# Sixteen projection quads in another matmul form: hi and lo of the activations in one matmul

## What is computed

```python
h = rmsnorm(x, g_pre_mix)
proj = h @ w_in                      # nq, nkv, ngate, rq, rk, rv, rg, mq, bg
mem_n = rmsnorm(mem, g_mem)
mkv = (mem_n @ w_mem_kv)             # memory keys and values
y_c = memory_attention(mq, mk, mv)   # 4 heads of 256
y_a = nsa_attention(q, kv, gates, ...)  # 8 heads of 128: compressed, selected, window
y_b = retention(q_r, k_r, v_r) * silu(rg)
merged = sum of sigmoid(bg[n]) * (y_n @ w_br_n)
x = x + rmsnorm(merged @ w_o, g_post_mix)
h2 = rmsnorm(x, g_pre_ffn)
x = x + rmsnorm((gelu(conv(h2 @ w_gate)) * conv(h2 @ w_val)) @ w_down, g_post_ffn)
```

## Time and profile before

| | us |
|---|---|
| median of 3 runs (lowest, highest) | 1719.74 (1719.73, 1719.93) |
| the profiled execution | 1719.76 |
| its span, first to last instruction | 1717.6 |
| PE busy with matmuls | 1703.9 |
| DVE busy | 1123.0 |
| ACT busy | 817.8 |

### The profile page before, as it was taken

How to read it: one execution, slowest core, us unless ns; L and a number is a source line. 1 busy time by engine, 2 the same in 40 slices (tenths; PEclk the granted TensorE clock), 3 DMA queues, 4 the chain that set the end, 5 groups by cost and what they waited for, 6 DMA issues and landing times.

```text
span 1717.6 us, 26440 instructions
## 1 busy us (share of the span) xinstructions
PE 1703.9 (99%) x9582; PEld 1494.4 (87%) x9582; DVE 1123.0 (65%) x1488; ACT 817.8 (48%) x1105; POOL 48.7 (3%) x53
## 2 busy tenths in 40 slices
PE   9999999999999999999999999999999999999997
PEld 9998999999888888888888888888888888888886
DVE  7645567666575554554565777776776776776777
ACT  7433345444344444444444565455455454454453
POOL 1000000000140000000000010000000000000000
PEclk9999999999999999999999999999999999999999
DMA  9566478444655666666657466666665666656654
GB/s 298 187 222 205 137 224 250 129 136 139 214 165 176 197 187 195 220 196 196 184 183 244 163 195 195 187 196 188 190 193 183 189 196 187 192 188 191 196 175 144
DMA packets 245992, 327.79 MB, mean 191 GB/s; under 512 B 12907, under 2 KB 167308, under 8 KB 245388
## 3 DMA queue, kind: packets, MB, share of 16 engines
q1 hardware_dynamic: 245900, 326.47, 61.0%
HBM read 321.71 MB, written 3.67 MB: 189 GB/s over the span
## 4 chain that ended last, share of the span: by engine, by line
PE 96%; DVE 1%; ACT 1%; issue 1%; DMA 1%; POOL 0%; POOLq 0%; DVEq 0%; SPq 0%; ACTq 0%
PE bank L1430 18%; PE bank L1421 15%; PE bank L1420 15%; PE bank L1422 15%; PE bank L1434 9%; PE bank L1394 4%; PE bank L1396 4%; PE bank L1395 4%; PE bank L1407 1%; PE bank L1409 1%; PE bank L1408 1%; PE bank L1728 0%; PE bank L1707 0%; PE bank L1646 0%; PE bank L1628 0%
## 5 line engine op out<-in xcount | busy, mean ns | idle before, releaser
L880 DVE TENSOR_TENSOR wlo<-wraw,whi 128x1024 fp32r<-128x1024 f32 x580 | 709.8, 1233 | 416.4 <-ACT whi L599 414.4
L599 ACT ACTIVATE whi<-wraw 128x1024 fp32r<-128x1024 f32 x580 | 611.9, 1059 | 653.4 <-PE bank L1422 378.3
L1430 PE MATMUL bank<-hx,whi 128*128 128x512 f32 x1376 | 344.6, 392 | 0.6 <-DVE wlo L880 0.5
L1430 PEld LDWEIGHTS bank<-hx,whi 128*128 128x128 f32 x1376 | 248.0, 189 | 45.9 <-issue 0.7
L1434 PEld LDWEIGHTS bank<-hx,wlo 128*128 128x128 f32 x1376 | 187.7, 190 | 13.4
L1434 PE MATMUL bank<-hx,wlo 128*128 128x256 f32 x1376 | 191.9, 282 | 0.0
L1420 PE MATMUL bank<-whi,hx 128*128 128x512 f32 x448 | 175.7, 392 | 0.0
L1422 PE MATMUL bank<-whi,hx 128*128 128x512 f32 x448 | 174.4, 389 | 0.0
L1421 PE MATMUL bank<-wlo,hx 128*128 128x512 f32 x448 | 174.3, 389 | 0.0
L1420 PE MATMUL bank<-whi,r_hi 128*128 128x512 f32 x384 | 149.8, 390 | 0.0
L1421 PE MATMUL bank<-wlo,r_hi 128*128 128x512 f32 x384 | 149.5, 389 | 0.0
(11 more groups left out here) (267 smaller groups left out, 2176.4 us busy)
## 6 DMA issues: line engine op xcount, KB each, us to landing
wraw<-in_w_in SPq DMA_DIRECT2D x200, 512.0 KB, 3.8
wraw<-in_w_up SPq DMA_DIRECT2D x176, 512.0 KB, 4.4
wraw<-in_w_down SPq DMA_DIRECT2D x88, 512.0 KB, 4.0
wraw<-in_w_mem_kv SPq DMA_DIRECT2D x32, 512.0 KB, 4.2
wraw<-in_w_o SPq DMA_DIRECT2D x32, 512.0 KB, 4.4
wraw<-in_w_br_mem SPq DMA_DIRECT2D x16, 512.0 KB, 4.3
wraw<-in_w_br_nsa SPq DMA_DIRECT2D x16, 512.0 KB, 4.5
wraw<-in_w_br_ret SPq DMA_DIRECT2D x16, 512.0 KB, 4.4
```

What stands on the lines that cost most here:

```text
L599: nc.scalar.activation(whi[:, c], wraw[:, c], ACT.Copy).then_inc(hi_done, 1)
L880: V.tensor_tensor(wlo[:, c], wraw[:, c], whi[:, c].bitcast(F32), ALU.subtract).then_inc(lo_done, 1)
L1430: T.matmul(ps[UP_PAIRS[j][t]][:, :], whi[:, c, k, t * P:(t + 1) * P], hx[:, :, k0 + k, :], start=first and k == 0, stop=False, skip_group_ ...
```

## The change

The sixteen quads of `mq`, `mk`, `nq`, `kv0` and of the second kv quad in `mix` go from `chunk_t` to a new `chunk_d`, which is `chunk_u` with the bank pair and the activations as arguments. The memory's hi and lo activations get one common tensor, `mx`. Each quad now takes a pair of banks. Their evacuation goes from `by_column` to `by_column_wide`, with a copy by ACT before it (`small`) into one buffer of 512 columns, `small_part`, which the next quad's copy may overwrite only when DVE has added it (`s_big`). The fourth part of the squares moves from the arena to `tables`, and the load of the bias tables waits for their last use (`s_fold`). The small products of the start move to banks 2 and 3, with waits on `evac[0]`, `s_rbc` and `s_gt` that the shared banks need. The order of the quads is not touched.

```diff
+MEM_PAIRS = ((0, 5), (1, 6), (4, 7))
+KEY_PAIRS = ((0, 5), (1, 7))
...
# ACT
+            def small(q, n, pair):
+                act.wait_ge(pe_done, 4 * q + 4)
+                if not (isinstance(n, int) and n == 0):
+                    act.wait_ge(s_big, n)
+                for u in range(2):
+                    e = nc.scalar.activation(small_part(n)[:, S * u:S * (u + 1)], bank(pair[u], 1), ACT.Copy)
+                e.then_inc(s_small, 1)
...
             for c in range(4):
                 square(0, c)
                 hi(1, c)
+            act.wait_ge(s_pad, 3)
+            small(0, 0, MEM_PAIRS[0])
             act.wait_ge(s_wg, 16)
-            act.wait_ge(s_pad, 3)
             nc.scalar.activation(gates(0), wgr[:, :, :], ACT.Copy).then_inc(s_wgh, 1)
             ahead(1)
+            small(1, 1, MEM_PAIRS[1])
             for c in range(4):
                 tiles_hi(m_hi, 1, c)
                 square(1, c)
                 if c >= 2:
                     ahead(2, (2 * (c - 2), 2 * (c - 2) + 1))
+            small(2, 2, MEM_PAIRS[2])
             act.wait_ge(s_gtt, 1)
...
-            ahead(3)
-            plain(Q0["mk"], 4)
+            for n in range(3, 8):
+                ahead(n, (0, 1, 2))
+                small(n, n, MEM_PAIRS[n % 2])
+                ahead(n, (3,))
+            plain(Q0["mv"], 2)
...
+            def ahead_and_small(q, n, pair):
+                ahead(q, (0, 1, 2))
+                small(q, n, pair)
+                ahead(q, (3,))
...
# DVE
+            def by_column_wide(q, b, n, pair, dst, r=0, scale=1.0, chunks=(0, 1, 2), late=(3,)):
+                ahead(q, chunks)
+                dve.wait_ge(s_small, n + 1)
+                for u in range(2):
+                    e = V.tensor_tensor(dst[:, S * u:S * (u + 1)], bank(pair[u], 0), small_part(n)[:, S * u:S * (u + 1)], ALU.add)
+                e.then_inc(s_big, 1)
+                dve.wait_ge(s_big, n + 1)
+                both = dst.rearrange("p (u s) -> p u s", u=2)
+                V.scalar_tensor_tensor(both, both, scale, rstd_rows(r).unsqueeze(1).to_broadcast([P, 2, S]),
+                                       ALU.mult, ALU.mult).then_inc(evac[b], 1)
+                ahead(q, late)
...
-            by_column(0, 0, arena[:, A_MQ:A_MQ + 512], 0, 1.0 / math.sqrt(MD), (), late=())
-            by_column(1, 1, arena[:, A_MQ + 512:A_MQ + 1024], 0, 1.0 / math.sqrt(MD), (), late=())
+            by_column_wide(0, 0, 0, MEM_PAIRS[0], arena[:, A_MQ:A_MQ + 512], 0, 1.0 / math.sqrt(MD), (), ())
+            by_column_wide(1, 1, 1, MEM_PAIRS[1], arena[:, A_MQ + 512:A_MQ + 1024], 0, 1.0 / math.sqrt(MD), (), ())
...
# PE
+            def chunk_d(q, c, pair, x2, k0, first, last):
+                pe.wait_ge(lo_done, 4 * q + (c + 1))
+                for k in range(CK):
+                    for u in range(2):
+                        T.matmul(ps[pair[u]][:, :], whi[:, c, k, u * P:(u + 1) * P], x2[:, :, k0 + k, :], start=first and k == 0,
+                                 stop=False, skip_group_check=True)
+                for k in range(CK):
+                    for u in range(2):
+                        e = T.matmul(ps[pair[u]][:, 0:S], wlo[:, c, k, u * P:(u + 1) * P], x2[:, 0, k0 + k, :], start=False,
+                                     stop=last and k == CK - 1, skip_group_check=True)
+                e.then_inc(pe_done, 1)
...
-            quad(chunk_t, 2, 5, 0, H, {0: lambda: rstd_to_rows(0)})
+            quad_d(2, 0, MEM_PAIRS[2], 0, hx, {0: lambda: rstd_to_rows(0)})
+            pe.wait_ge(evac[0], 1)
...
+            def memory_sums():
+                pe.wait_ge(s_rbc, 1)
+                token_sums(1)
+            quad_d(3, 1, MEM_PAIRS[1], 1, hx, {1: gates_to_tokens, 2: memory_sums})
...
-                quad(chunk_t, Q0["mk"] + n, n % 2, (G0["mk"] + n) // 2, MM, {0: lambda: rstd_to_rows(1)} if n == 0 else {})
+                quad_d(Q0["mk"] + n, n % 2, MEM_PAIRS[n % 2], (G0["mk"] + n) // 2, mx, {0: lambda: rstd_to_rows(1)} if n == 0 else {})
+            pe.wait_ge(s_gt, 1)
```

More of the change, by code:

```diff
@@ L151, in build @@
         h_hi, h_lo = hx[:, 0], hx[:, 1]
-        m_hi, m_lo = (sb(n, [P, KT, S], F32R) for n in ("m_hi", "m_lo"))
+        mx = sb("mx", [P, 2, KT, S], F32R)
+        m_hi, m_lo = mx[:, 0], mx[:, 1]
         r_hi, r_lo = (sb(n, [P, 8 * S + P], F32R) for n in ("r_hi", "r_lo"))
@@ L241, in by_feature, with small_part @@
             return arena[:, 4096 * n:4096 * (n + 1)].rearrange("p (k s) -> p k s", k=KT)
+        def small_part(n):
+            return arena[:, A_SMALL:A_SMALL + 512]
         def squared(c):
+            if c == 3:
+                return tables[:, 0:1024]
             return arena[:, A_SQ + 1024 * c:A_SQ + 1024 * (c + 1)]
@@ L392, in _ @@
             sp.wait_ge(s_scr, 16)
+            sp.wait_ge(s_fold, 2)
             sp.dma_start(tables[:, :].rearrange("p (h n) -> p h n", h=HEADS),
@@ L661, in _ @@
                     e.then_inc(m_ex, 1)
-                    ahead(q)
+                    ahead(q, (0, 1, 2))
+                    small(q, 2 * i + (j + 8), KEY_PAIRS[j])
+                    ahead(q, (3,))
                     act.wait_ge(m_o, m + 2)
                     nc.scalar.activation(m_hi[:, bass.ds(2 * m, 2), :], bank(6), ACT.Copy).then_inc(m_h, 1)
-            ahead(Q0["kv0"])
-            ahead(Q0["kv0"] + 1)
+            def ahead_and_small(q, n, pair):
+                ahead(q, (0, 1, 2))
+                small(q, n, pair)
+                ahead(q, (3,))
+            for n in range(2):
+                ahead_and_small(Q0["kv0"] + n, 12 + n, KEY_PAIRS[n])
             for n in range(2):
@@ L669, in _ @@
                 nc.scalar.activation(blocks(n, 0), wblocks(n), ACT.Copy).then_inc(s_bkh, 1)
-            ahead(Q0["kv0"] + 2)
+            ahead_and_small(Q0["kv0"] + 2, 14, KEY_PAIRS[0])
             for m, part in enumerate(MIX):
                 q = Q0["mix"] + m
+                if part == ("kv", 1):
+                    ahead_and_small(q, 15, KEY_PAIRS[0])
+                    continue
                 ahead(q, (0,))
@@ L966, in _ @@
             fold_rest()
-            by_column(2, 0, arena[:, A_MQ + 1024:A_MQ + 1536], 0, 1.0 / math.sqrt(MD), (), 5, ())
+            by_column_wide(2, 0, 2, MEM_PAIRS[2], arena[:, A_MQ + 1024:A_MQ + 1536], 0, 1.0 / math.sqrt(MD), (), ())
             dve.wait_ge(s_br, 1)
-            V.tensor_copy(work[:, W_ROW:W_ROW + REL], ps[4][:, 0:REL]).then_inc(s_rbc, 1)
+            V.tensor_copy(work[:, W_ROW:W_ROW + REL], ps[3][:, 0:REL]).then_inc(s_rbc, 1)
             dve.wait_ge(s_gp, 1)
-            V.tensor_tensor(work[0:48, W_SIG:W_SIG + S], ps[7][0:48, 0:S], rstd_rows(0)[0:48], ALU.mult).then_inc(s_gc, 1)
+            V.tensor_tensor(work[0:48, W_SIG:W_SIG + S], ps[2][0:48, 0:S], rstd_rows(0)[0:48], ALU.mult).then_inc(s_gc, 1)
             mean_square(1)
@@ L974, in _ @@
             V.tensor_scalar(sig[:, :, :], sig[:, :, :], 0.5, 0.5, ALU.mult, ALU.add).then_inc(s_sig, 1)
-            by_column(3, 1, arena[:, A_MQ + 1536:A_MQ + 2048], 0, 1.0 / math.sqrt(MD), (0, 1, 2), 6)
+            by_column_wide(3, 1, 3, MEM_PAIRS[1], arena[:, A_MQ + 1536:A_MQ + 2048], 0, 1.0 / math.sqrt(MD))
             rows_out(1)
-            with dve.Fori(0, 2) as i:
-                for j in range(2):
-                    by_column(2 * i + (Q0["mk"] + j), j, arena[:, bass.ds(1024 * i + (A_MK + 512 * j), 512)], 1)
+            for n in range(4):
+                by_column_wide(Q0["mk"] + n, n % 2, 4 + n, MEM_PAIRS[n % 2], arena[:, A_MK + 512 * n:A_MK + 512 * (n + 1)], 1)
             for i in range(2):
@@ L1014, in _ @@
             for n, dst in enumerate((A_KC, A_VC)):
-                by_column(Q0["kv0"] + n, n, arena[:, dst:dst + 512])
+                by_column_wide(Q0["kv0"] + n, n, 12 + n, KEY_PAIRS[n], arena[:, dst:dst + 512])
             dve.wait_ge(evac[0], G0["kv0"] // 2 + 1)
@@ L1029, in _ @@
                 V.tensor_tensor(blocks(n, 1), wblocks(n), blocks(n, 0).bitcast(F32), ALU.subtract).then_inc(s_bkl, 1)
-            by_column(Q0["kv0"] + 2, 0, arena[:, A_KS:A_KS + 512])
+            by_column_wide(Q0["kv0"] + 2, 0, 14, KEY_PAIRS[0], arena[:, A_KS:A_KS + 512])
             for m, (kind, n) in enumerate(MIX):
@@ L1532, in quad, with quad_d @@
                         between[c]()
+            def quad_d(q, b, pair, before, x2, between={}, tiles_ready=None):
+                if -1 in between:
+                    between[-1]()
+                bank_free(b, before)
+                for c in range(4):
+                    if tiles_ready is not None:
+                        pe.wait_ge(tiles_ready[0], tiles_ready[1] + 2 * c + 2)
+                    chunk_d(q, c, pair, x2, 4 * c, c == 0, c == 3)
+                    if c in between:
+                        between[c]()
             def group(q, chunks, i, phase, x_, between={}, tiles_ready=None):
@@ L1598, in _ @@
                 w = wg[:, 48 * k:48 * k + P]
```

(13 more changed lines are left out.)

17 lines of the change are left out of this document (9 added, 8 removed).

## The result

The changed kernel takes 1722.99 us in the median of 17 runs (1721.56 to 1724.16), the kernel before 1719.87 in as many (1719.58 to 1720.28). The ratio is 1.0016, with a 95% interval from 1.0009 to 1.0023. The change costs 3.1 us, where 1719.7 and a range from 1716.3 to 1722.6 were predicted. The changed kernel also spreads over 2.6 us, the one before over 0.7.

What follows compares the result with a forecast made beforehand. PE's matmul stream was taken to bound the kernel: 6.0 gained less 3.6, 1.4 and 1.0 us lost waiting on other engines gives 0.0, so 1719.7 us, with a range from 1716.3 to 1722.6.

Steps and rivals of the forecast that it cites:

- B: Second mix quad: DVE's later start delays the compression blocks, splits and loads PE waits for; cost 1.4 us, bounds 0.7 to 1.8.
- C: Two compression quads behind the mix's key quad: DVE bounds them and starts later; cost 1.0 us, bounds 0.7 to 1.3.
- The gain on PE: Sixteen changed quads: chunks take 2.791 us instead of 2.885, as in the up projection; gain 6.0 us.
- Place A: Fourth memory query quad: PE stops 3.4 us for the gates by token; total cost 3.6 us, bounds 2.4 to 4.6.
- ACT's stop: At the start, ACT's second small copy waits for DVE's add for the first quad; memory tiles start at R + 2.45.
- R: Start time of PE's product `rstd_to_rows(0)`, 35.85 us in the kernel before, from which the late chain is counted.
- The lowered clock: Rival, chance 0.14: the stop in quad 3 lowers the clock; one stretch costs 2.2 us and gives 1721.9, two 1724.1.
- the bounds of the costs: All three places together: costs between 3.8 and 7.7 us, giving 1717.5 to 1721.5 us.

Runs made afterwards that it cites:

- experiment 3: Changed kernel with eleven matmuls of 512 columns into an unused bank ahead of PE's wait for the gates by token: 1720.29 us.
- experiment 1: Changed kernel with the second quad's small-part copy on ACT moved behind the first memory tiles and squares: 1721.44 us.
- experiments 9 and 10: Kernel before, no quad changed, with spare DVE operations ahead of the bias-row copy and gate operation: three (9) 1724.58 us, two (10) 1723.30 us.
- experiment 4: Changed kernel with only the second kv0 quad back in the old form and evacuation: 1721.34 us.
- Experiment 5: Changed kernel with only the mix's key quad back in the old form and evacuation: 1722.56 us.
- the seventh: Changed kernel with DVE's gate operation made earlier and the second kv0, third kv0 and mix's key quads in the old form: 1716.22 us.
- experiment 10: Kernel before, no quad changed, with two spare DVE operations ahead of the bias-row copy and gate operation: 1723.30 us.

## Why the prediction was wrong

The step that failed is the clock: the prediction forecast the pause of 3.4 us and put nothing into its sum for a lowered clock behind it. The runs show that price as 1.6 us in the profiled execution and about 2.7 in the median.

In the profiled execution the sum of the stages closes within the span: 1717.6 - 5.2 (gain) + 3.3 (pause) + 1.6 (clock) + 1.5 (B) + 1.2 (the third mix quad) + 0.9 (C) = 1720.9, measured 1721.0. The 0.3 us by which the time around the span has shrunk lie in no stage; the kernels with the new form all show it (1.8 to 1.9 us around the span), and it stays unexplained. In the median, with the clock at the 2.7 us of experiment 3 and the third mix quad left out, 1719.9 - 5.2 + 3.3 + 2.7 + 1.5 + 0.9 - 0.3 = 1722.8 for 1722.99; the 2.7 come from this median, so this sum tests little.

- **The gain on PE**, forecast 6.0, was 5.5 by the plain stretch and 5.2 by all stages. The 2.791 us of the up projection were not the pitch in the changed quads, 2.799. A little of that is its first chunk, which follows another form directly and takes 2.76; the other 15 still give 2.793, and the rest of the difference is not explained.
- **Place A, size**: right. A pause of 3.4 us was forecast, 3.3 is there, at the foreseen instruction.
- **Place A, cause**: wrong in the main. The forecast began its chain with ACT's stop, and the chain came as forecast (the gates' product at R + 22.6, forecast R + 22.7). But experiment 1 took 2.5 us off that stop and got 0.5 us. DVE was 96% busy in this stretch already before, and three wide evacuations add 2.5 us to its work up to the gates; that queue stood only 0.5 us behind ACT's chain. The number came out since the chain I summed ran over the same DVE operations.
- **The lowered clock**: the step that failed. It was a rival with 0.14, because the trace before had no pause of that length; "no row of before tests it" was taken as little chance instead of as an open question. The forecast was missed by 3.3 us, and experiment 3, which keeps PE at work in the pause, takes 2.7 us away; experiments 9 and 10 show that the pause is enough, without the new form. The price from the earlier trace rows, 2.2 us, lies among the measured ones (1.5 to 2.9 us from profile to profile, none in experiment 4).
- **Places B and C**: 1.4 and 1.0 forecast, 1.5 and 0.9 measured. Experiment 5 shows C; experiment 4 shows 0.8 of B, and the seventh that 0.5 more goes with the third kv0 quad.
- **The third mix quad**: 1.2 us in the profile, not forecast; what made the loads late in that execution stays open.
- **The chances**: given a forecast pause of over 3 us, the time to forecast was the one with the clock, 1719.7 + 2.2 = 1721.9 us. The range's upper end, 1722.6, also took that price alone, without the bounds of the costs on top of it; the result lies 0.4 us beyond.

The Trainium skill's rule in "TensorE: Matmul & The Clock Gate", section "Why this matters for your kernels", that idle gaps of PE between bursts lower the clock, agrees with these traces in all but one (experiment 4, whole after 3.2 us), and it was there to be weighed.

## What to carry to other kernels

When a change makes an engine other than PE late in one place, price the pause twice, once as itself and once as the clock behind it, also where the kernel before never paused. Before blaming a wait on one engine, look how full the window of the engine behind it was already: here DVE, at 96%, passed the 2.5 us of added work on in full. And a form that saves PE 3% of a quad by giving the others four more operations belongs where they have room: 14 quads with the gates moved gain 3.9 us, all 16 as they stand lose 3.1.

## What the runs showed of the hardware

After pauses of PE of 2.0, 2.7 and 3.1 to 3.2 us the granted clock fell to the 1.2 GHz level, after 0.3 and 0.7 us it didn't, and in one of the profiles with 3.2 us (experiment 4) it didn't either: how long it is low differs between executions with the same pause (1.6 or 2.9 us lost behind 3.2), and by the single runs of experiment 10 so does whether it falls. It came back by itself within some 3.5 to 7 us while PE went on working. In the record of the kernel's start the clock reads 1.00 while ten matmuls of 512 columns take 0.44 us each; that is their pace at the lowered clock in the changed kernel too (eight in 3.52 us). So there the lower level is likely and the record doesn't show it, but no run here tests that.
